# A normalisation turn laid out by feature block: one eviction of 512 or 256 columns in place of four of 128

## The chip, the cores and the metric

One NeuronCore of a Trainium2 chip runs the whole program in one launch. The metric is the device time of that launch in microseconds (us), the median of several runs. Inside the core, TensorE (PE in the profile) multiplies and transposes, VectorE (DVE) and ScalarE (ACT) compute and bring results out of PSUM, GpSimd (POOL) helps, and SyncE (SP) issues most of the DMA transfers. PSUM has eight banks of 512 float32 columns.

## What is computed

Two blocks of a model run behind each other on 512 image tokens and 256 context tokens of width 1024, all in float32. The first block mixes the tokens (a gated delta rule in both directions beside a convolution module) and then sends the image tokens through 64 experts, six for each token. The second block has an RWKV layer and a latent-attention layer. Each of these four layers begins in the same way, and this is the part the change is about:

```python
def rmsnorm(x, g):
    xf = x.astype(jnp.float32)
    y = xf * lax.rsqrt(jnp.mean(xf * xf, axis=-1, keepdims=True) + EPS)
    return (y * g.astype(jnp.float32)).astype(x.dtype)

def modulate(h, shift, scale):
    return h * (1 + scale) + shift

        h_x = rmsnorm_2(x, norm_g[i]) * (1.0 + sc_x) + sh_x
        h_c = rmsnorm_2(ctx, norm_g[i]) * (1.0 + sc_c) + sh_c
```

The inverse length belongs to a token, gain and shift belong to a feature, and the context has a gain and a shift of its own.

## The kernel before, in words

The tokens lie in `K.X` as six tiles of 128 tokens by 1024 features: tiles 0 and 1 are the context, 2 to 5 the image. The layers behind want the features on the partitions, `K.hT[feature in block, block k, token]` with `KD` = 8 blocks of 128 features. `norm_turn` makes the one out of the other. It is called four times: ahead of `mixer_inputs` with six tiles, ahead of `router` with the four image tiles, ahead of `rwkv_heads` with six, and ahead of `mla_inputs` with six. In the views the tile of scaled tokens is `norm_xn`, and the inverse lengths (`known`) were made by the layer before.

The program is a row of phases written by hand. `phase` opens a block in which each engine has a program of its own, and a barrier of all engines stands between two blocks (its branches are the lines L61 and L63 of the views). So nothing of the next phase starts on any engine until the last one has finished the turn. DMAs that SP issued inside a phase go on across the barrier; each turn is given a function `ahead`, which issues the loads for the phase behind it.

The turn before goes tile by tile. DVE multiplies a tile by its inverse lengths (L472) into one of two buffers. PE transposes its eight blocks of 128 by 128 (L497) into two of four banks; a bank then holds four feature blocks of one tile. As gain and shift differ from block to block, each of the eight blocks is evicted by an instruction of its own, 128 columns wide: ACT takes blocks 0 to 3 (L456), DVE blocks 4 to 7 (L483). DVE's order is this:

```python
            scale(0)
            for n, j in enumerate(tiles):
                if n + 1 < N:
                    scale(n + 1)
                r = int(j < JC)
                dve.wait_ge(S["turned"], n + 1)
```

and `scale(n)` waits until the transposes of tile n-2 have given its buffer back. PE waits for the scaled tile and, from the third tile on, for both evictions of the tile two before.

## Time and profile before

| | before |
|---|---|
| median of 3 runs | 2966.68 us (2965.19 to 2973.23) |
| profiled execution, its own time | 2958.97 us |
| its span | 2957.3 us |
| PE busy | 2529.8 us, 86% |
| DVE busy | 1372.4 us, 46% |
| ACT busy | 709.6 us, 24% |
| POOL busy | 458.9 us, 16% |
| HBM read and written | 413.82 and 76.55 MB |

The span is the time between the first and the last instruction of the profiled execution; its own time lies 1.67 us above it. Busy shares are averages over very different layers. What a stretch between two barriers costs is read from its own rows, not from these shares.

### The profile page before, as it was taken

To read this page: it belongs to the slowest core of one execution; us is meant where nothing else is said; L and a number is where in the kernel's file an instruction comes from. 1 tells how busy PE (TensorE), PEld (TensorE's weight loads), DVE (VectorE), ACT (ScalarE), POOL (GpSimd) and SP (SyncE) were. 2 spreads that over 40 slices of the span, in tenths; PEclk is the share of its full clock that TensorE was granted. 3 is DMA by queue.
4 is the path that set the end of the run, shared out by engine and by line. 5 is a ranking of instruction groups with operands and counts; after the bars stand their busy time and mean duration, and the time that the engine had idled before them with its cause. 6 is when DMAs were issued, how large, how long until landed. Compare 5 with 4: busy or idle time off the path is not lost. (4 is left out here: it accounts for less than half of the span.)

```text
span 2957.3 us, 48668 instructions
## 1 busy us (share of the span) xinstructions
PE 2529.8 (86%) x19642; PEld 1482.0 (50%) x19642; DVE 1372.4 (46%) x2761; ACT 709.6 (24%) x1320; POOL 458.9 (16%) x426
## 2 busy tenths in 40 slices
PE   5999773988899998997179999979998499989988
PEld 2554353954444443433045556458887145545553
DVE  1550646533611111111887885966665562034442
ACT  3111340102111111111324641133333113134441
POOL 0000132300111111111000000022211220035450
PEclk8999876998999999999599999999999799999999
DMA  6110611015589999995615655244443932021001
GB/s 250 51 57 1 218 21 27 7 58 183 211 323 394 389 416 404 401 389 212 234 61 145 161 141 173 111 132 133 127 125 84 359 114 95 6 40 18 15 29 64
DMA packets 328930, 471.43 MB, mean 159 GB/s; under 512 B 151465, under 2 KB 225107, under 8 KB 304005
## 3 DMA queue, kind: packets, MB, share of 16 engines
q1 hardware_dynamic: 302645, 373.92, 36.6%
q10 hardware_dynamic: 12960, 69.21, 5.7%
q0 software_dynamic: 13104, 25.19, 2.3%
q8 instruction: 158, 2.59, 0.4%
q14 instruction: 63, 0.52, 0.1%
HBM read 413.82 MB, written 76.55 MB: 166 GB/s over the span
## 5 line engine op out<-in xcount | busy, mean ns | idle before, releaser
L1962 PE MATMUL psum<-ex_w,hT 128*64 128x512 f32 (+1 forms) x1104 | 329.3, 617 | 26.4 <-DMA ex_w<-in_exp_w_up 24.7
L1962 PEld LDWEIGHTS psum<-ex_w,hT 128*64 128x64 f32 (+1 forms) x1104 | 124.9, 158 | 224.6 <-issue 222.5
L4005 POOL TENSOR_SCALAR mla_pool<-mla_pool,at_stats 128x768 f32<-128x768 f32 x64 | 140.2, 2203 | 252.4 <-DVE at_stats L4023 252.4
L2195 DVE COPY slot_act_t<-psum 128x256 f32<-128x256 f32 x45 | 19.1, 424 | 325.2 <-PE psum L1970 325.2
L560 PE MATMUL psum<-hT,weights 128*128 128x512 f32 x384 | 166.8, 592 | 0.0
L1978 PE MATMUL psum<-ex_w,slot_act_t 128*64 128x512 f32 (+1 forms) x552 | 163.4, 597 | 1.4 <-DVE slot_act_t L2195 1.4
L1947 POOL DMA_INDIRECT scratch_ys<-slot_out,slot_row x45 | 45.3, 1006 | 465.3 <-issue 401.6
L560 PEld LDWEIGHTS psum<-hT,weights 128*128 128x128 f32 x384 | 73.0, 190 | 86.6 <-issue 86.0
L2151 ACT ACTIVATE slot_silu<-psum 128x256 f32<-128x256 f32 x45 | 17.3, 384 | 397.6 <-PE psum L1962 397.6
L497 PE MATMUL psum<-const,norm_xn 128*128 128x128 f32 x176 | 30.0, 332 | 91.8 <-DVE norm_xn L472 91.8
L3903 PE MATMUL psum<-mla_kT,at_qT 128*128 128x512 f32 (+1 forms) x256 | 93.3, 489 | 2.6 <-DVE at_qT L4015 1.6
L3179 PE MATMUL psum<-rs_r_ident,rs_b 64*32 64x96 f32 x1536 | 83.8, 249 | 13.6 <-POOL rs_k_ident L3151 12.9
L1978 PEld LDWEIGHTS psum<-ex_w,slot_act_t 128*64 128x64 f32 (+1 forms) x552 | 55.8, 153 | 75.8 <-issue 71.2
L2202 DVE COPY slot_out<-psum 128x512 f32<-128x512 f32 x45 | 31.1, 692 | 128.8 <-PE psum L1978 128.8
L4028 DVE TENSOR_REDUCE at_stats<-psum 128x1 f32<-128x768 f32 x64 | 61.1, 955 | 61.8 <-PE psum L3903 61.6
L3978 ACT ACTIVATE mla_pool<-psum,at_stats 128x768 f32<-128x768 f32 x64 | 57.6, 901 | 127.6 <-DVE at_stats L4033 127.5
L2762 PE MATMUL psum<-rh_w,rh_lerp 128*128 128x256 f32 (+1 forms) x288 | 85.0, 458 | 3.2 <-ACT rh_xx L2837 2.7
L3472 PE MATMUL psum<-ro_wo,ro_oT 128*128 128x512 f32 x192 | 86.4, 608 | 0.9 <-DMA ro_wo<-in_rwkv_w_out 0.9
L2696 PE MATMUL psum<-rh_lerp,rh_w 128*128 128x512 f32 (+1 forms) x256 | 86.2, 490 | 0.0
L3179 PE MATMUL psum<-rs_r_ident,rs_k_ident 64*32 64x96 f32 x1536 | 84.3, 249 | 1.2 <-issue 1.1
L2658 PE MATMUL psum<-rh_lerp,rh_w 128*128 128x512 f32 (+1 forms) x256 | 83.9, 486 | 0.7 <-issue 0.7
L2762 PE MATMUL psum<-tokens,rh_lerp 128*128 128x512 f32 x192 | 82.7, 592 | 0.0
(573 smaller groups left out, 4996.4 us busy)
## 6 DMA issues: line engine op xcount, KB each, us to landing
ex_w<-in_exp_w_gate SPq DMA_DIRECT2D x64, 1024.0 KB, 9.1
ex_w<-in_exp_w_up SPq DMA_DIRECT2D x64, 1024.0 KB, 18.9
ex_w<-in_exp_w_down ACTq DMA_DIRECT2D x60, 1024.0 KB, 10.3
mod_ring<-in_w_mod SPq DMA_DIRECT2D x12, 2048.0 KB, 13.3
scratch_features<-tokens SPq DMA_DIRECT2D x96, 256.0 KB, 3.8
weights<-in_w_in SPq DMA_DIRECT2D x6, 2048.0 KB, 8.1
ex_w<-in_mod_w SPq DMA_DIRECT2D x6, 2048.0 KB, 12.5
ex_w<-scratch_ys SPq DMA_DIRECT2D x8, 1536.0 KB, 18.8
```

The costliest lines, as they stand in the source:

```text
L560: mm = pe.matmul(K.bank[2 * (f % 4)][:, :], K.wring[:, n % RING, k, m * P:(m + 1) * P], K.hT[:, k, TC:TT], start=(k == 0), stop=(k == KD - 1))
L1962: mm = pe.matmul(bank[at:at + n, :], XT[:, k, at:at + n], W[:, 0:2, k * DE:(k + 1) * DE], start=(k == 0), stop=(k == KD - 1))
L1978: mm = pe.matmul(bank[at:at + n, :], aT[:, m, at:at + n], W[:, 2, m * D + h * 512:m * D + (h + 1) * 512], start=(m == 0), stop=(m == 1))
L2658: mm = pe.matmul(K.bank[b][:, 0:t1 - t0], rk_w(s)[:, 1, k, :], lerp[:, 0, k, t0:t1], start=(k == 0), stop=(k == KD - 1))
L2696: mm = pe.matmul(K.bank[2 + seg][:, 0:t1 - t0], rk_w(s)[:, 0, k, :], lerp[:, 1, k, t0:t1], start=(k == 0), stop=(k == KD - 1))
L2762: mm = pe.matmul(K.bank[u % 4][:, 0:cols], lerp[:, n, k, j * P:(j + 1) * P], w[:, k, :], start=(k == 0), stop=(k == KD - 1))
L3179: m = pe.matmul(K.bank[scb(u, k)[p]][sides[p], ch * P:ch * P + W], lhs[p], RI[part, k, ch, :], start=True, stop=True)
L3472: mm = pe.matmul(K.bank[M_[j % 2][half]][:, :], oT[:, j % 2, k, :], wb[:, k, half * 512:(half + 1) * 512], start=(k == 0), stop=(k == KD - 1))
L3903: mm = pe.matmul(K.bank[2 * (u % 2) + b][:, 0:t1 - t0], qT[:, s, h, qt * P:(qt + 1) * P], kT[:, s, h, t0:t1], start=True, stop=True)
L3978: act.activation(Pm[:, q % 2, u, :], K.psum[:, b * 512:b * 512 + TT], ACT.Exp, bias=st[:, 1, u:u + 1], scale=SCALE, accum_out=st[:, 2, u:u ...
L4005: pool.tensor_scalar(Pm[:, q % 2, u, :], Pm[:, q % 2, u, :], st[:, 3, u:u + 1], None, ALU.mult)\
L4028: dve.tensor_reduce(st[:, 0, u:u + 1], K.psum[:, b * 512:b * 512 + TT], AX.X, ALU.max)\
```

## The change

The turn goes by feature blocks. All tiles get a buffer of their own, so that they can be scaled without waiting: DVE scales tiles 0, 2, 4 and ACT tiles 1, 3, 5. PE first transposes the two context tiles into banks 0 to 3, where the two tiles of one feature block stand side by side (256 columns). Then it goes through the eight feature blocks of the image tiles: the four tiles of one block fill one bank (512 columns), in banks 4 to 7 and then 0 to 3, which by then have to be evicted. One instruction evicts one feature block, since all of its columns share gain and shift: 256 columns wide for the context, 512 for the image, half of them on ACT and half on DVE. Three of the calls pass `room`: memory that is unused at that time serves for some or all of the buffers. The branch that computed the inverse lengths within the turn, which no caller used, is gone.

```diff
--- before.py
+++ after.py
@@ -418,20 +418,27 @@
 
 
 
-def norm_turn(K, tiles, gain, shift, known=None, ahead=None):
+def norm_turn(K, tiles, gain, shift, known, ahead=None, room=()):
+
 
 
     nc = K.nc
-    names = "sq_done rms_done inv_done xn_done turned evac_a evac_b"
+    N, ctx = len(tiles), [n for n, j in enumerate(tiles) if j < JC]
+    names = "xn_v xn_a turned evac_v evac_a"
     with ExitStack() as c, phase(nc, names) as (block, S):
-        if known is None:
-            junk = c.enter_context(sbuf(nc, "norm_junk", [P, D], F32))
-            ssq, rms, inv = (c.enter_context(sbuf(nc, "norm_" + n, [P, NT], F32)) for n in ("ssq", "rms", "inv"))
-        xn = c.enter_context(sbuf(nc, "norm_xn", [P, 2, D], F32))
-        N = len(tiles)
-
-        def bank(n, half):
-            return K.bank[2 * (n % 2) + half]
+        xn = list(room)[:N]
+        if len(xn) < N:
+            own = c.enter_context(sbuf(nc, "norm_xn", [P, N - len(xn), D], F32))
+            xn += [own[:, n, :] for n in range(N - len(xn))]
+        parts = [(k, 1) for k in range(KD) if ctx] + [(k, 0) for k in range(KD)]
+        turned = lambda k, r: (k // 2 + 1) * 2 if r else k + 1 + (KD if ctx else 0)
+        on_dve = lambda k, r: (k // 2 if r else k) % 2
+        x_bank = lambda k: (4 + k) % 8
+
+        def source(k, is_ctx):
+            if is_ctx:
+                return K.bank[k // 2][:, (k % 2) * TC:(k % 2 + 1) * TC], K.hT[:, k, 0:TC]
+            return K.bank[x_bank(k)][:, :], K.hT[:, k, TC:TT]
 
         if ahead:
             @block.sync
@@ -440,61 +447,45 @@
 
         @block.scalar
         def _(act):
-            if known is None:
-                for n, j in enumerate(tiles):
-                    if n:
-                        act.wait_ge(S["sq_done"], n)
-                    act.activation(junk[:, :], K.X[:, j, :], ACT.Square, accum_out=ssq[:, n:n + 1])\
-                        .then_inc(S["sq_done"], 1)
-                act.wait_ge(S["sq_done"], N)
-                act.activation(rms[:, 0:N], ssq[:, 0:N], ACT.Sqrt, bias=K.eps[:, :], scale=1.0 / D)\
-                    .then_inc(S["rms_done"], 1)
-            for n, j in enumerate(tiles):
-                r = int(j < JC)
-                act.wait_ge(S["turned"], n + 1)
-                for k in range(KD // 2):
-                    last = act.activation(K.hT[:, k, j * P:(j + 1) * P], bank(n, 0)[:, k * P:(k + 1) * P],
-                                          ACT.Identity, bias=shift[:, k, r:r + 1], scale=gain[:, k, r:r + 1])
-                last.then_inc(S["evac_a"], 1)
+            for n in range(1, N, 2):
+                act.activation(xn[n], K.X[:, tiles[n], :], ACT.Copy, scale=known[:, n:n + 1]).then_inc(S["xn_a"], 1)
+            for k, r in parts:
+                if not on_dve(k, r):
+                    act.wait_ge(S["turned"], turned(k, r))
+                    bank, out = source(k, r)
+                    act.activation(out, bank, ACT.Identity, bias=shift[:, k, r:r + 1], scale=gain[:, k, r:r + 1])\
+                        .then_inc(S["evac_a"], 1)
 
         @block.vector
         def _(dve):
-            if known is None:
-                dve.wait_ge(S["rms_done"], 1)
-                dve.reciprocal(inv[:, 0:N], rms[:, 0:N]).then_inc(S["inv_done"], 1)
-                dve.wait_ge(S["inv_done"], 1)
-            scales = inv if known is None else known
-
-            def scale(n):
-                if n >= 2:
-
-                    dve.wait_ge(S["turned"], n - 1)
-                dve.tensor_scalar(xn[:, n % 2, :], K.X[:, tiles[n], :], scales[:, n:n + 1], None, ALU.mult)\
-                    .then_inc(S["xn_done"], 1)
-
-            scale(0)
-            for n, j in enumerate(tiles):
-                if n + 1 < N:
-                    scale(n + 1)
-                r = int(j < JC)
-                dve.wait_ge(S["turned"], n + 1)
-                for k in range(KD // 2, KD):
-                    q = k - KD // 2
-                    last = dve.tensor_scalar(K.hT[:, k, j * P:(j + 1) * P], bank(n, 1)[:, q * P:(q + 1) * P],
-                                             gain[:, k, r:r + 1], shift[:, k, r:r + 1], ALU.mult, ALU.add)
-                last.then_inc(S["evac_b"], 1)
+            for n in range(0, N, 2):
+                dve.tensor_scalar(xn[n], K.X[:, tiles[n], :], known[:, n:n + 1], None, ALU.mult).then_inc(S["xn_v"], 1)
+            for k, r in parts:
+                if on_dve(k, r):
+                    dve.wait_ge(S["turned"], turned(k, r))
+                    bank, out = source(k, r)
+                    dve.tensor_scalar(out, bank, gain[:, k, r:r + 1], shift[:, k, r:r + 1], ALU.mult, ALU.add)\
+                        .then_inc(S["evac_v"], 1)
 
         @block.tensor
         def _(pe):
-            for n in range(N):
-                pe.wait_ge(S["xn_done"], n + 1)
-                if n >= 2:
-
-                    pe.wait_ge(S["evac_a"], n - 1)
-                    pe.wait_ge(S["evac_b"], n - 1)
+            def ready(n):
+                pe.wait_ge(S["xn_a"] if n % 2 else S["xn_v"], n // 2 + 1)
+
+            for n in ctx:
+                ready(n)
                 for k in range(KD):
-                    half, q = divmod(k, KD // 2)
-                    tr = pe.transpose(bank(n, half)[:, q * P:(q + 1) * P], xn[:, n % 2, k * P:(k + 1) * P], K.ident)
+                    at = (k % 2) * TC + n * P
+                    tr = pe.transpose(K.bank[k // 2][:, at:at + P], xn[n][:, k * P:(k + 1) * P], K.ident)
+                    if n == ctx[-1]:
+                        tr.then_inc(S["turned"], 1)
+            for k in range(KD):
+                if ctx and x_bank(k) < 4:
+                    pe.wait_ge(S["evac_v"] if x_bank(k) % 2 else S["evac_a"], x_bank(k) // 2 * 2 + 2)
+                for q, n in enumerate(range(len(ctx), N)):
+                    if k == 0:
+                        ready(n)
+                    tr = pe.transpose(K.bank[x_bank(k)][:, q * P:(q + 1) * P], xn[n][:, k * P:(k + 1) * P], K.ident)
                 tr.then_inc(S["turned"], 1)
 
 
@@ -2460,7 +2451,7 @@
                 mods.request(I, sp)
 
             norm_turn(K, range(JC, NT), K.mods[:, 1, 0, :, :], K.mods[:, 1, 1, :, :], K.inv,
-                      ahead=ahead)
+                      ahead=ahead, room=[Wb[:, 0, :, :].rearrange("p w n -> p (w n)")[:, n * D:(n + 1) * D] for n in range(JX)])
             router(K, I, wt, kept, R, rw, bias, mods, Wb, shared)
         dispatch(K, wt, kept, w_of, extra, order, h_rows, idx, to_row, Wb, src, acc, mods, K.next_mods,
                  scratch["gate_rows"], steps, Hg, G)
@@ -4074,6 +4065,7 @@
                 ws = sb("ml_w", [P, KD, SMALL], c3)
                 N = held(nc, c3, "w_in g_in0 g_in1")
                 norm_turn(K, range(NT), K.mods[:, 0, 0, :, :], K.mods[:, 0, 1, :, :], K.inv,
+                          room=[pool_[:, (8 + n) * D:(9 + n) * D] for n in range(4)],
                           ahead=lambda sp: load_latents(I, sp, N, ws, gate_weights(pool_)))
                 dump(K, dbg, "hh1", K.hT[:, :, :])
                 qc = pool_[:, 10752:12288].rearrange("p (j n) -> p j n", j=JX)
@@ -4166,7 +4158,9 @@
                     K.hT = sb("hT", [P, KD, TT], c3)
                     K.wring = sb("weights2", [P, RING, KD, WCH], c3)
                     W = held(nc, c3, MIXER_SEMS)
-                    norm_turn(K, range(NT), K.mods[:, 0, 0, :, :], K.mods[:, 0, 1, :, :], inv,
+                    free = [headsT[:, 2 * n:2 * n + 2, :].rearrange("p a t -> p (a t)") for n in range(4)] +\
+                        [cfa[:, 2 * n:2 * n + 2, :].rearrange("p a t -> p (a t)") for n in range(2)]
+                    norm_turn(K, range(NT), K.mods[:, 0, 0, :, :], K.mods[:, 0, 1, :, :], inv, room=free,
                               ahead=lambda sp: [load_mixer(K, I, sp, W, n) for n in range(RING)])
                     dump(K, dbg, "hT", K.hT[:, :, :])
                     mixer_inputs(K, I, C, zT, cfa, cfs, ba[:, :, :], W)
```

The next rows are PE's instructions in the first turn, before the change; `const` is the identity, and what stands in square brackets are the semaphores that the instruction waits for.

```order
L497 MATMUL psum<-const,norm_xn 128x128 [waits xn_done]
L497 MATMUL psum<-const,norm_xn 128x128 x7
L497 MATMUL psum<-const,norm_xn 128x128 [waits xn_done]
L497 MATMUL psum<-const,norm_xn 128x128 x7
L497 MATMUL psum<-const,norm_xn 128x128 [waits evac_b,evac_a,xn_done]
L497 MATMUL psum<-const,norm_xn 128x128 x7
```

The last two rows stand there for each of the tiles 2 to 5. With the change PE has this at the same place (`mix_heads` and `cf_a` are the memory passed as `room`; the buffers of tiles 0 to 3 lie in the first, those of 4 and 5 in the second):

```order
L479 MATMUL psum<-const,mix_heads 128x128 [waits xn_v]
L479 MATMUL psum<-const,mix_heads 128x128 x7
L479 MATMUL psum<-const,mix_heads 128x128 [waits xn_a]
L479 MATMUL psum<-const,mix_heads 128x128 x7
L488 MATMUL psum<-const,mix_heads 128x128 [waits xn_v]
L488 MATMUL psum<-const,mix_heads 128x128 [waits xn_a]
L488 MATMUL psum<-const,cf_a 128x128 [waits xn_v]
L488 MATMUL psum<-const,cf_a 128x128 [waits xn_a]
L488 MATMUL psum<-const,mix_heads 128x128 x2
L488 MATMUL psum<-const,cf_a 128x128 x2
```

There are 48 transposes in both. Before, four of the six groups wait for evictions; now the waits for scaled tiles stand in the first twenty, and the 28 behind them wait only four times, once for each of banks 0 to 3. In the turn with four image tiles the 16 rows of L479 and these four waits are missing.

The next rows are DVE's in the first turn, before the change.

```order
L472 TENSOR_SCALAR norm_xn<-tokens,norm_inv 128x1024 x2
L483 TENSOR_SCALAR hT<-psum,mod_cols 128x128 [waits turned]
L483 TENSOR_SCALAR hT<-psum,mod_cols 128x128 x3
L472 TENSOR_SCALAR norm_xn<-tokens,norm_inv 128x1024 [waits turned]
L483 TENSOR_SCALAR hT<-psum,mod_cols 128x128 [waits turned]
L483 TENSOR_SCALAR hT<-psum,mod_cols 128x128 x3
```

And these are DVE's with the change:

```order
L462 TENSOR_SCALAR mix_heads<-tokens,norm_inv 128x1024 x2
L462 TENSOR_SCALAR cf_a<-tokens,norm_inv 128x1024
L467 TENSOR_SCALAR hT<-psum,mod_cols 128x256 [waits turned] x4
L467 TENSOR_SCALAR hT<-psum,mod_cols 128x512 [waits turned] x4
```

Before, scaling a tile stood behind the eviction of the tile two ahead of it, and DVE had 24 evictions and six scalings. Now its three scalings stand first and wait for nothing, and eight evictions follow. ACT's list changes in the same way: 24 evictions of 128 columns become three scalings, four evictions of 256 columns and four of 512.

## Rows read from the trace of the kernel before

**Rows 1.** Busy time by engine in the four turns, first scaling to last eviction

```profile
core 0: us, PE busy (x) PEld busy (x) DVE busy (x) ACT busy (x) POOL busy (x), PEclk, DMA share, GB/s
60.14:73.48 13.34, 7.66 (x48) 6.49 (x48) 11.81 (x30) 8.91 (x24) 0.00 (x0) 0.87 0.94 338
687.22:696.44 9.22, 5.62 (x32) 4.74 (x32) 7.93 (x20) 6.01 (x16) 0.00 (x0) 0.81 0.50 133
1461.10:1474.45 13.35, 8.31 (x48) 6.97 (x48) 11.81 (x30) 9.02 (x24) 0.00 (x0) 0.79 0.72 167
2467.87:2481.21 13.34, 8.39 (x48) 7.05 (x48) 11.81 (x30) 9.02 (x24) 0.00 (x0) 0.79 0.94 354
```

**Rows 2.** Timeline of the first turn: start, length, engine, line, idle before

```profile
60.14 1.42 DVE L472 TENSOR_SCALAR norm_xn<-tokens,norm_inv 128x1024 f32<-128x1024 f32 x2 [0.84 <-PEq L63]
60.95 3.29 PE L497 MATMUL psum<-const,norm_xn 128*128 128x128 f32 x16 [2.08 <-DVE norm_xn L472]
...
70.85 1.09 PE L497 MATMUL psum<-const,norm_xn 128*128 128x128 f32 x8 [0.84 <-DVE norm_xn L472]
71.98 1.50 ACT L456 ACTIVATE hT<-psum,mod_cols 128x128 f32<-128x128 f32 x4 [0.43 <-PE psum L497]
...
74.32 5.19 PE L556 MATMUL psum<-hT,weights 128*128 128x256 f32 x16 [2.38 <-PEq L63]
```

**Rows 3.** Timeline of PE in the last turn and behind it

```profile
2468.68 3.68 PE L497 MATMUL psum<-const,norm_xn 128*128 128x128 f32 x16 [2.34 <-DVE norm_xn L472]
...
2482.02 18.30 PE L3679 MATMUL psum<-ml_w,hT 128*128 128x384 f32 x56 [2.35 <-PEq L63]
```

**Rows 4.** Stretches in and behind the turns; PEclk is the granted clock's share

```profile
61.00:63.00 2.00, 2.00 (x10) 2.00 (x11) 0.60 (x2) 0.04 (x1) 0.00 (x0) 0.50 0.79 193
64.00:73.00 9.00, 4.61 (x35) 3.44 (x33) 9.00 (x26) 7.38 (x21) 0.00 (x0) 1.00 1.05 392
74.00:77.00 3.00, 2.68 (x6) 2.18 (x7) 0.00 (x0) 0.00 (x0) 0.21 (x4) 0.50 1.05 386
...
2469.00:2473.00 4.00, 3.58 (x17) 3.19 (x16) 2.60 (x8) 2.11 (x6) 0.00 (x0) 0.50 0.93 336
2474.00:2481.00 7.00, 3.48 (x26) 2.57 (x24) 7.00 (x19) 5.80 (x16) 0.00 (x0) 1.00 1.04 409
...
688.50:691.00 2.50, 2.50 (x13) 2.50 (x12) 1.35 (x5) 1.21 (x4) 0.00 (x0) 0.50 0.71 156
...
699.00:709.00 10.00, 10.00 (x49) 10.00 (x49) 0.00 (x0) 1.60 (x3) 0.00 (x0) 0.50 1.03 372
```

**Rows 5.** Groups of instructions by form: count, busy us, mean ns of one

```profile
L2912 DVE TENSOR_SCALAR rh_sq<-psum 128x512 f32<-128x512 f32 x8 | 5.5, 691 | 44.6 <-PE psum L2668 44.6
L2786 ACT ACTIVATE rh_a<-psum,rh_cols 128x512 f32<-128x512 f32 x16 | 11.0, 688 | 0.1
L2379 ACT ACTIVATE junk<-tokens 128x1024 f32<-128x1024 f32 x10 | 10.6, 1057 | 57.7 <-DVE tokens L2425 57.5
```

**Rows 6.** Line L497: ns of one transpose, min/median/max

```profile
L497 PE MATMUL psum<-const,norm_xn x176: 272/273/477, 61.0 to 2479.4; 128*128 128x128 f32 x176
```

**Rows 7.** DMAs that feed the phases behind: KB each, us from issue to landing

```profile
weights<-in_w_in SPq DMA_DIRECT2D x1, 2048.0 KB, 8.1
...
ml_w<-in_mla_w_in SPq DMA_DIRECT2D x1, 2688.0 KB, 9.9
```

**Rows 8.** Timeline behind the second turn (router)

```profile
697.25 12.66 PE L1586 MATMUL psum<-rt_w,hT 128*128 128x64 f32 x64 [2.35 <-PEq L63]
...
697.81 1.28 ACT L1600 ACT_TABLE_LOAD   x1 [1.37 <-POOL ex_w L1576]
```

**Rows 9.** Timeline behind the third turn (RWKV)

```profile
1475.25 0.45 DVE L2877 COPY rh_xx<-hT 128x8 f32<-128x8 f32 x1 [0.94 <-PEq L63]
...
1478.99 5.31 PE L2725 MATMUL psum<-rh_lerp,rh_exps 128*128 128x512 f32 x8 [6.09 <-DVE rh_lerp L2888]
```

**Rows 10.** The costliest group of the page, section 5 (experts)

```profile
L1962 PE MATMUL psum<-ex_w,hT 128*64 128x512 f32 (+1 forms) x1104 | 329.3, 617 | 26.4 <-DMA ex_w<-in_exp_w_up 24.7
```

## The prediction

> **What bounds the kernel now.** I read the stretches of the four turns first. Each turn lies between two barriers, so its length is on the path whatever the busy shares of the whole program say. The three turns of six tiles take 13.34, 13.35 and 13.34 us, that of four takes 9.22 us: 49.3 us, 1.7% of the span [rows 1]. That is the most that the change can touch directly. Inside a turn no engine is at its limit: in the first, PE is busy 7.66 us of 13.34, DVE 11.81, ACT 8.91 [rows 1]. The timeline then shows the loop that sets the pace: eight transposes take 1.09 us, and before them PE was idle for 0.84 us, waiting for DVE to have scaled the tile [rows 2]. So a tile takes 1.93 us, and DVE is the late one: its scaling of a tile stands in its queue behind four evictions of 128 columns. The last eviction, ACT's, starts at 71.98 and ends at 73.48; the next phase's first matmul starts 0.84 us later, at 74.32 [rows 2]. This 0.84 us is the barrier and stays.
>
> **What a turn takes with the change.** Take t as the time since the first scaling starts.
>
> Start: PE starts at 60.95, 0.81 us after DVE [rows 2]; unchanged, as tile 0 is scaled by the same instruction.
>
> Scaled tiles: two scalings on DVE take 1.42 us [rows 2], so tiles 0, 2, 4 are ready at about 0.8, 1.4 and 2.2. ACT's scaling of 1024 columns isn't in the trace; the nearest row is an ACT pass over the same columns out of SBUF, 1.06 us [rows 5], so tiles 1, 3, 5 are ready at 1.1, 2.2 and 3.2. From below it can't be faster than DVE's 0.71, which would change nothing with six tiles. From above, a table load of 1.28 us [rows 8] might come ahead of it; then tile 5 is ready at 4.5. PE needs it after 19 transposes, at 0.81 + 19 x 0.213 = 4.9 at the low clock and at 4.1 if the clock rises as in the first turn. With six tiles that is covered to within 0.4 us; with four it would cost up to 1.3 us. The evictions that ACT runs before go without a load, and I take none.
>
> Transposes: the same 48. One lasts 273 ns at best and 477 at worst [rows 6]. Eight in 1.09 us [rows 2] make (1.09 - 0.27) / 7 = 0.117 us from start to start; sixteen in 3.68 us [rows 3] make (3.68 - 0.48) / 15 = 0.213. The granted clock explains the two: 0.50 (1.2 GHz) from 2469 to 2473 and from 61 to 63, then 1.00 (2.4 GHz) for the rest of the turn [rows 4]. So the clock rose 2 to 3 us after PE's first transpose in the first turn and 4.3 to 5.3 us after it in the last [rows 2 to 4]. What PE does in that time is nearly the same with the change (transposes back to back), and I take the same rises, 2.4 and 4.6 us. The third turn has the same busy times as the last [rows 1] and gets the same number.
>
> Evictions: DVE's 512 columns out of PSUM with scalars took 0.69 us, ACT's with one operand by pointer 0.69 us [rows 5]; ACT's here has two, which I put at up to 0.78. One bank of image columns takes PE 4 x 0.117 = 0.47 us at its fastest, so each engine gets a bank every 0.94 us and keeps up. Nor do PE's four new waits bind: the context banks are full at t = 4.2 at the latest, ACT has taken the first two of its four (under 0.69 us each) by about 4.6, DVE its own by the same time, and PE reaches the first of these banks with transpose 33, at t = 5.6 in the first turn and 6.6 in the others. The last bank is DVE's. The tail is therefore 0.15 us for the last transpose to end and 0.04 + 0.69 for its eviction: 0.88.
>
> Six tiles, third and last turn: 0.81 + 4.6 at the low clock (21.6 transposes) + 26.4 x 0.117 = 3.1 + 0.88 = 9.4 us, 3.9 less than 13.3. First turn: 0.81 + 2.4 (11.3 transposes) + 36.7 x 0.117 = 4.3 + 0.88 = 8.4, 4.9 less. Four tiles: the first bank waits for ACT's second scaling and is full at 2.4; low to about 4.6 (clock 0.50 from 688.5 to 691 [rows 4]), 10 transposes; 18 more take 2.1; with the tail 7.6, 1.6 less than 9.2.
>
> **What the saved time runs into.** The transfers for the next phase are issued as the turn begins and don't get faster. The mixer's first weights land 8.1 us after issue, `ml_w` after 9.9 [rows 7]. The mixer's PE would now start at t = 8.4 + 0.84 = 9.2, 1.1 us after the landing; that of the latent projections at 10.2, 0.3 us after it. Both are still hidden, the second just so: if that turn is shorter than I say, the DMA takes the rest. Behind the third turn DVE has to work first, from 1475.25 to 1478.99, before PE gets its first operand [rows 9], so all of the saving there passes on. The router's matmuls begin as the barrier opens and wait for no DMA [rows 8].
>
> Behind the turns the clock matters too. The mixer's first 16 matmuls took 5.19 us, most of it at 0.50 [rows 2, 4]; PE will have paused for less time, and up to 1.5 us (half of 2.9) may come back. The router's 64 matmuls took 12.66 us [rows 8] at 0.50 [rows 4]; at the transposes' 0.117 they would take 7.5, 5.2 less. The last turn's followers ran at 18.30 / 56 = 0.327 us each, with the clock at 1.00 ahead of them [rows 3, 4], and could lose 1.5 us by a start like the mixer's. I take zero for all three.
>
> **The sum.** 4.9 + 1.6 + 3.9 + 3.9 = 14.3 us. The profiled execution's own 2958.97 us becomes 2944.7. The median of the runs, 2966.68, lies 7.7 above that execution, so in terms of the median I forecast 2952.4. About 0.3%, 8.9 us, is what a measurement of this kernel can tell from no change (its three runs lie 8 us apart).
>
> **Rivals.** (1) The clock never rises in a turn laid out like this. Then 48 transposes take 0.81 + 48 x 0.213 + 0.88 = 11.9 us, 1.4 saved three times, and the four-tile turn takes 2.4 + 28 x 0.213 + 0.88 = 9.2, nothing saved: 4.2 us in all, 2962.5. Against it: from 64 to 73 and from 2474 to 2481 PE ran nothing but transposes, in bursts, and was granted 1.00 [rows 4]. This is what the Trainium skill would have ("TensorE: Matmul & The Clock Gate", section "Part 4: PE-mode transpose"): it says that the full clock does not engage for transposes, because they don't count as work in the same way. By that rule the sum would be 4.2 in place of 14.3; the trace contradicts it. Chance 0.04.
>
> (2) The saving is given back further on. The costliest group, the experts' matmuls, was kept waiting 24.7 us by weights [rows 10]; if the arrival of those didn't move with the start, the 6.5 us of the first two turns would be lost there, which leaves 7.8: 2958.9. Against it: these loads are issued by phases behind the same barriers, which move forward as a whole. Chance 0.13.
>
> (3) More than forecast: the router's stage keeps the high clock and the mixer starts on it. 14.3 + 5.2 + 1.5 = 21, 2945.7. For it: PE is denser before the barrier. Against it: in the router's stage 10 us of unbroken matmuls of 64 columns did not bring the clock up again [rows 4], so it would only be held for a while. Chance 0.13.
>
> (4) Slower: a stream behind a turn stays at 1.2 GHz as the router's did. Only the 56 matmuls behind the last turn are long enough: all of them at half speed cost 18.3 us more, and the change turns into a loss once more than 14.3 us of that stream, four fifths of it, ran low; in full it gives 2970.7. Against it: this stream ran at 0.327 us each from its first matmul, and PE's pause ahead of it gets no longer. Chance 0.03.
>
> **How the numbers follow.** The forecast case, savings of 9 to 18 us, has 0.67. The range of 2945 to 2961 holds it, case 3 and most of case 2; it leaves out cases 1 and 4 and some of the spread of the runs. Faster by over 0.3%: nearly all of the forecast case, case 3 and a little of case 2, 0.80. Within 0.3%: case 1, most of case 2 and the lower edge of the forecast case, 0.17. Slower: 0.03.
>
> **What the profile after would show.** The turns at 8.4, 7.6, 9.4 and 9.4 us from the first scaling to the last eviction; PE without a gap in its transposes from the twentieth on, at 0.117 us each after the clock's rise; evictions of 512 columns at 0.69 to 0.78 us; no ACT_TABLE_LOAD in a turn; the matmuls behind the last turn waiting for no DMA. The prediction is wrong if PE waits for evictions in banks 0 to 3, if the clock rises later than before, or if a phase behind a turn doesn't end earlier by as much as the turn did.

## The result, and the profile after

The changed kernel takes 2945.11 us (median of 10 runs, 2938.78 to 2958.05) where the kernel before takes 2966.17 (10 runs, 2962.28 to 2975.91). The ratio is 0.9927, with a 95% interval of 0.9915 to 0.9938: about 21 us faster. I had forecast 14.3; the median lies at the lowest edge of my range, 2945 to 2961. The profiled execution took 2945.34 us, its span is 2943.6. In three of the later experiments one run of twelve took 5.4 to 8.0 ms, far off all others, and is left out of the ratio.

The four turns in the trace after, from the first scaling to the last eviction, against [rows 1] (columns: length of the stretch, busy us and count of each engine, granted clock, DMA share and GB/s):

```profile
60.02:68.75 8.73, 7.07 (x48) 6.84 (x48) 7.03 (x11) 8.03 (x11) 0.00 (x0) 0.76 0.88 313
683.30:691.34 8.04, 6.11 (x32) 5.29 (x32) 4.65 (x6) 5.27 (x6) 0.00 (x0) 0.66 0.43 100
1451.76:1460.93 9.17, 7.51 (x48) 7.28 (x48) 7.23 (x11) 8.26 (x11) 0.00 (x0) 0.72 1.05 237
2457.70:2467.36 9.66, 8.00 (x48) 7.76 (x48) 7.22 (x11) 8.25 (x11) 0.00 (x0) 0.69 0.90 333
```

They took 13.34, 9.22, 13.35 and 13.34 us before, so the turns themselves give 4.6, 1.2, 4.2 and 3.7, together 13.7 us. PE now works 7.1 to 8.0 us of the 8.7 to 9.7 in the turns of six tiles; DVE has 11 instructions where it had 30.

The groups of the first turn by form (count, busy us, mean ns of one) show the new operations; they answer to [rows 5]:

```profile
L467 DVE TENSOR_SCALAR hT<-psum,mod_cols 128x512 f32<-128x512 f32 x4 | 3.1, 805 | 0.1
L456 ACT ACTIVATE hT<-psum,mod_cols 128x512 f32<-128x512 f32 x4 | 3.0, 782 | 0.2
L456 ACT ACTIVATE hT<-psum,mod_cols 128x256 f32<-128x256 f32 x4 | 1.9, 562 | 0.0
L467 DVE TENSOR_SCALAR hT<-psum,mod_cols 128x256 f32<-128x256 f32 x4 | 1.9, 537 | 1.6 <-PE psum L479 1.6
L451 ACT ACTIVATE cf_a<-tokens,norm_inv 128x1024 f32<-128x1024 f32 x1 | 1.1, 1132 | 0.0
```

What lies behind the turns is the part that I had not counted. The timeline of the changed kernel, behind the first turn, from the second turn's transposes on, and behind the last turn, is to be read beside [rows 2, 8]:

```profile
69.59 3.69 PE L547 MATMUL psum<-hT,weights 128*128 128x256 f32 x16 [1.68 <-PEq L63]
...
685.52 4.98 PE L488 MATMUL psum<-const,ex_w 128*128 128x128 f32 x29 [0.27 <-ACT ex_w L451]
...
692.18 7.33 PE L1577 MATMUL psum<-rt_w,hT 128*128 128x64 f32 x64 [1.68 <-PEq L63]
...
703.88 3.65 PE L246 MATMUL psum<-ex_w 128*64 128x512 f32 x16 [0.79 <-DMA ex_w<-in_mod_w]
...
2468.19 14.11 PE L3670 MATMUL psum<-ml_w,hT 128*128 128x384 f32 x43 [1.68 <-PEq L63]
```

The router's 64 matmuls take 7.33 us where they took 12.66, and the mixer's first 16 take 3.69 where they took 5.19. The stretches of the changed kernel give the reason, against the last rows of [rows 4]: the granted clock is 1.00 (2.4 GHz) through both, where it was 0.50 (1.2 GHz) in nearly all of both.

```profile
684.00:688.00 4.00, 3.62 (x15) 3.03 (x16) 1.52 (x3) 2.51 (x4) 0.00 (x0) 0.50 0.51 112
689.00:691.00 2.00, 1.50 (x14) 1.26 (x12) 1.67 (x3) 1.55 (x2) 0.00 (x0) 1.00 0.49 108
692.00:699.00 7.00, 6.82 (x61) 6.85 (x62) 0.11 (x1) 2.79 (x3) 0.52 (x1) 1.00 1.04 391
69.60:73.00 3.40, 3.40 (x16) 3.01 (x17) 0.00 (x0) 0.00 (x0) 0.16 (x4) 1.00 1.05 386
```

In the trace of before the router's matmuls, from 697.25 on, did not meet a low clock. They met a high one and lost it 1.3 us later:

```profile
697.25:698.55 1.30, 1.30 (x12) 1.30 (x13) 0.11 (x1) 0.74 (x1) 0.48 (x1) 1.00 1.05 405
698.65:709.90 11.25, 11.25 (x56) 11.13 (x55) 0.00 (x0) 1.95 (x3) 0.00 (x0) 0.50 1.03 374
```

To see where the whole difference lies, I split each span into four stretches and the rest. A stretch begins with DVE's first scaling of a turn and ends where the phase behind it has passed the point in question: for the mixer, the start of its first 512-column matmul; for the router, the first matmul of the dispatch phase; for RWKV and the latent projections, their first matmul. In us:

| trace | mixer | router | RWKV | latent | sum | rest of the span |
|---|---|---|---|---|---|---|
| before | 19.2 | 40.9 | 17.9 | 14.1 | 92.2 | 2865.1 |
| before, second trace | 19.8 | 41.2 | 17.9 | 14.1 | 93.0 | 2871.6 |
| changed | 13.1 | 34.1 | 13.9 | 10.5 | 71.7 | 2871.9 |
| changed, second | 13.5 | 34.1 | 14.5 | 10.1 | 72.2 | 2866.0 |
| changed, third | 13.0 | 33.9 | 14.7 | 10.6 | 72.2 | 2871.3 |
| changed, fourth | 13.2 | 33.9 | 13.8 | 9.7 | 70.6 | 2867.3 |

The sums differ by 20 to 22 us, which is the measured gain. The two first spans differ by 13.7 only, because the rest of the program, whose instructions the change doesn't touch, was 7 us shorter in the first trace of before than in the first of the changed kernel. Over the 18 traces of this study the rest lies between 2865.1 and 2876.7.

A part of that rest does answer to the turns. The first 56 matmuls of the latent projections took 18.30 us in all four traces of the changed kernel, at a granted clock of 1.00. In the five traces with the old turn ahead of them they took 18.30, 19.93, 19.99, 21.35 and 21.26 us; only the first trace of before, the one that I had read, had no low clock in them. In the second one the clock was low for their first 3 us:

```profile
2487.90:2491.00 3.10, 3.10 (x5) 1.75 (x6) 1.04 (x6) 0.00 (x0) 1.27 (x1) 0.50 1.05 410
2491.20:2507.00 15.80, 15.80 (x51) 9.33 (x50) 0.00 (x0) 2.88 (x9) 0.00 (x0) 1.00 0.08 29
```

### The profile page after: what moved, and what is told of

Same layout as the page of the kernel before. It is cut to its first block and busy times, and to the rows that moved or that the text cites. A ratio compares the mean times of both kernels' runs of the same rounds, so it can differ in the third digit from the quotient of the medians.

```text
span 2943.6 us, 48528 instructions
## 1 busy us (share of the span) xinstructions
PE 2529.8 (86%) x19642; PEld 1482.2 (50%) x19642; DVE 1355.8 (46%) x2690; ACT 706.8 (24%) x1271; POOL 459.3 (16%) x426
## 5 line engine op out<-in xcount | busy, mean ns | idle before, releaser
L3170 PE MATMUL psum<-rs_r_ident,rs_b 64*32 64x96 f32 x1536 | 84.4, 249 | 13.1 <-POOL rs_k_ident L3142 12.8
L246 PE MATMUL psum<-mod_ring,mod_silu 128*64 128x512 f32 x192 | 54.9, 724 | 31.6 <-DMA mod_ring<-in_w_mod 29.2
```

Of the source, the lines that this page charges most:

```text
L3170: m = pe.matmul(K.bank[scb(u, k)[p]][sides[p], ch * P:ch * P + W], lhs[p], RI[part, k, ch, :], start=True, stop=True)
```

## The experiments

All ratios are to the kernel before, run on the same chip in the same session. A kernel without a ratio had one execution.

**The kernel before again.** No edit.

> The kernel before, unchanged. If the measured ratio of 0.9927 is all of the change, this gives a ratio of 1.000 within 0.001. It also gives a second trace of the kernel before. Theory 1 (the part of the gain that was not forecast is the clock behind the turns): the router's 64 matmuls take 12.7 us again, and the first 16 of the mixer 5.2 us. Rival (the first trace of before was a lucky one, and a usual execution is longer somewhere else): some stretch outside the turns is longer by several us than in the first trace, and the span is nearer 2964 than 2957.

Measured: ratio 1.0000 (0.9988 to 1.0012), span 2964.7. The router's matmuls took 12.58 us:

```profile
701.10 12.58 PE L1586 MATMUL psum<-rt_w,hT 128*128 128x64 f32 x64 [2.34 <-PEq L63]
```

Both sides were right in a part. The clock behind the turn is as low as in the first trace, and the first trace of before was a short one, by 7.4 us, all but 0.8 of it in the rest of the table. So a difference of two spans says little here, and a difference of stretches does.

**The new turn ahead of the router alone, and in the other three places alone.**

```diff
-            norm_turn(K, range(JC, NT), ...
+            norm_turn_before(K, range(JC, NT), ...   # second kernel; the first has the three others so
```

> The new turn ahead of the router alone, the old one in the three turns of six tiles. Theory 1: the turn itself gives 1.2 us and the router's matmuls on the high clock 5.3, together 6.5 us (ratio 0.9978). Rival (the router's clock is chance and does not come with the turn): 1.2 us, ratio 0.9996, and the router's matmuls take 12.7 us in the trace.

> The new turn in the three places with six tiles, the old one ahead of the router. Theory 1: the turns give 4.6 + 4.2 + 3.7 = 12.5 us and the mixer's start 1.5, together 14.0 us (ratio 0.9953); with the run before this it adds up to the change. Rival (savings are given back or multiplied elsewhere): the two ratios don't add up to 0.9927 within 0.002.

Measured: 0.9970 (0.9959 to 0.9982) for the router alone and 0.9948 (0.9932 to 0.9965) for the other three. The two savings, 0.0030 and 0.0052, add up to 0.0082 beside 0.0073 for the change, within their intervals. The router's matmuls took 7.33 us with its own new turn and 12.26 us without it:

```profile
698.57 7.33 PE L1659 MATMUL psum<-rt_w,hT 128*128 128x64 f32 x64 [1.68 <-PEq L63]
```

```profile
696.02 12.26 PE L1659 MATMUL psum<-rt_w,hT 128*128 128x64 f32 x64 [2.35 <-PEq L63]
```

A turn that became 1.5 us shorter (7.69 for 9.22) is worth 8.9 us (3.4 either way), and the stretch by itself 6.8 to 7.1. The rival, that the router's clock doesn't come with the turn, falls.

**Spare matmuls in the old turn of the router.** The kernel before; PE does work in its pauses whose results nobody uses.

```diff
                 tr.then_inc(S["turned"], 1)
+                if N == JX:
+                    for i in range((0, 1, 3, 7)[n]):
+                        pe.matmul(K.bank[7][:, :], K.ident, K.const[:, 0:512], start=True, stop=True)
```

> The kernel before with 11 spare matmuls of 512 columns in PE's idle time of the router's turn (1 behind the second tile, 3 behind the third, 7 behind the last), their results unused. The turn itself stays as long as before, 9.2 us. Theory 1 (a denser PE ahead of the barrier keeps the clock for the router): the 64 matmuls take about 7.3 us instead of 12.7 and the kernel gains about 5 us (ratio 0.998). Rival (what keeps the clock is something else, or the 64-column matmuls lose it anyway): they take 12.7 us and the ratio is 1.000.

```profile
695.11 6.17 PE L501 MATMUL psum<-const 128*128 128x512 f32 x14
702.14 7.33 PE L1589 MATMUL psum<-rt_w,hT 128*128 128x64 f32 x64 [0.86 <-PEq L63]
```

The clock was kept, 7.33 us, but the ratio is 1.0010 (0.9998 to 1.0022). The row above shows my mistake: the last seven matmuls stand there as fourteen and take 6.17 us, 0.88 each. The last eviction ended after 11.6 us instead of 9.2, and PE's spare work held the barrier for longer still: the router's first matmul came 16.9 us after the first scaling (702.14, from 685.26) instead of 10.0. What the stage gained, the turn and the wait for the spare matmuls lost; the stretch is 41.3 us, as long as in the kernel before. I repeated it with three: 256 columns behind the third tile, 512 and 256 behind the last.

> The kernel before with fewer spare matmuls in the router's turn, since in the run with 11 of them each took 0.88 us and the turn got 2.3 us longer: now one of 256 columns behind the third tile and one of 512 and one of 256 behind the last, results unused. Theory 1 (the clock behind the turn is decided by how busy PE is ahead of the barrier): the turn takes 9.2 to 9.5 us and the 64 router matmuls 7.3 us, ratio 0.998. Rival (so little work is not enough, or it was the shorter pause ahead of the stage): the matmuls take 12.6 us, ratio 1.000.

```profile
695.32 1.46 PE L501 MATMUL psum<-const 128*128 128x512 f32 x4
697.83 7.33 PE L1589 MATMUL psum<-rt_w,hT 128*128 128x64 f32 x64 [1.05 <-PEq L63]
```

The turn took 9.47 us, the matmuls 7.33, and the router's stretch 34.7 us instead of 41.2. So an old turn with a busier PE, and with a pause of 1.05 us instead of 2.35, gives the stage behind it the same clock as the new one. Which of the two did it, this run doesn't tell. The ratio is 0.9990 (0.9978 to 1.0001). That is 3 us (0 to 6.5) where the stretch says 6.5: at the edge of the interval, so the mechanism is shown by the trace, its worth in the median only roughly.

**A buffer for every tile and scaling on two engines, in the old layout.**

```diff
-            scale(0)
+            for n in range(0, N, 2):
+                dve.tensor_scalar(xn[n], K.X[:, tiles[n], :], known[:, n:n + 1], None, ALU.mult).then_inc(S["xn_v"], 1)
             for n, j in enumerate(tiles):
-                if n + 1 < N:
-                    scale(n + 1)
...
```

(against the kernel before; ACT scales tiles 1, 3, 5 in the same way, and PE waits for the scaled tiles of either)

> A buffer for every tile and scaling on both engines up front, as in the change, but the old layout in PSUM with 128-column evictions tile by tile. Theory 1 (the layout with wide evictions and the early scaling are both needed): DVE and ACT then work 12 and 8 evictions less nothing, that is each engine still has 24 evictions of 0.32 to 0.375 us behind its three scalings; ACT is the last with 3.2 + 24 x 0.375 = 12.2 us, a turn of six takes 12.3 us, 1.1 less than before, and half of the gain behind the turns may come: ratio 0.998. Rival (the loop scale, transpose, evict was the whole cost): turns of 9.5 us, ratio 0.993.

Turns of 11.56, 8.47, 12.10 and 11.55 us, ratio 0.9990 (0.9979 to 1.0000). The router's 64 matmuls took 11.90 us, so their clock was lost as before. ACT's row in the last turn shows the new pace: it evicts without a pause, 0.35 us for each 128 columns, while PE waits for it.

```profile
2469.90 8.45 ACT L449 ACTIVATE hT<-psum,mod_cols 128x128 f32<-128x128 f32 x24
```

**The new layout with evictions of 128 columns.**

```diff
-                    act.activation(out, bank, ACT.Identity, ...).then_inc(S["evac_a"], 1)
+                    for at in range(0, TC if r else TX, P):
+                        last = act.activation(out[:, at:at + P], bank[:, at:at + P], ACT.Identity, ...)
+                    last.then_inc(S["evac_a"], 1)
```

(and the same on DVE)

> The changed kernel, but each feature block is evicted by instructions of 128 columns again (two for the context, four for the image), on the same engine as with the change. Theory 1: each engine has 24 of them behind its three scalings, the turn of six tiles ends at about 12.2 us as in the run with the old layout, the one of four at 2.2 + 16 x 0.375 = 8.2 to 8.6; PE waits for evictions in banks 0 to 3. Ratio to before 0.998. Rival: the evictions hide behind PE at the low clock and the ratio is that of the change, 0.993.

Turns of 11.72, 9.64, 11.72 and 11.73 us, ratio 0.9988 (0.9977 to 1.0000). The last turn's rows on PE and ACT:

```profile
2483.82 0.38 PE L492 MATMUL psum<-const,norm_xn 128*128 128x128 f32 x2
2488.94 3.54 PE L3674 MATMUL psum<-ml_w,hT 128*128 128x384 f32 x5 [4.75 <-PEq L63]
```

```profile
2479.66 8.48 ACT L457 ACTIVATE hT<-psum,mod_cols 128x128 f32<-128x128 f32 x24
```

PE is through at 2484.2 and then stands for 4.75 us; ACT's 24 evictions end at 2488.1. I had expected PE to be held up in banks 0 to 3; it was not, the evictions only come out behind it. The start of the latent projections after so long a pause is slow as well, 0.7 us for each of five. The router's matmuls took 13.65 us. Both experiments scale ahead and evict 128 columns at a time; they differ in the layout. Early scaling is thus worth about 3 us by the median with either layout (7 to 8 us by the four stretches with the old one, 2 to 3 with the new one; they add up to 85.1 and 90.2 us), and widening the evictions on top of it brings the gain to 21. Wide evictions without the early scaling were not run: one bank takes a block of four tiles, so those tiles have to be scaled first.

**All scaling on DVE.**

```diff
-            for n in range(1, N, 2):
-                act.activation(xn[n], K.X[:, tiles[n], :], ACT.Copy, scale=known[:, n:n + 1]).then_inc(S["xn_a"], 1)
...
-            for n in range(0, N, 2):
+            for n in range(N):
                 dve.tensor_scalar(xn[n], K.X[:, tiles[n], :], known[:, n:n + 1], None, ALU.mult).then_inc(S["xn_v"], 1)
```

> The changed kernel with all tiles scaled by DVE. Theory 1 (the scaling on ACT is hidden): DVE scales six tiles in 4.1 us, tile 5 is ready at 4.1 us where PE needs it at 4.9, so the turns of six tiles change by less than 0.3 us; DVE's evictions then start 2 us later, up to 0.5 us more at the end. In the turn of four the last tile is ready at 2.8 instead of 2.2, 0.2 us more. Ratio 0.993 within 0.001. Rival (the two-engine scaling is a main part of the gain): turns 2 us longer, ratio 0.996.

Turns of 9.75, 9.76, 9.63 and 8.75 us, ratio 0.9952 (0.9939 to 0.9965), above the 0.993 that I had expected to within 0.001. The turns of six tiles are 1.0 and 0.5 us longer and 0.9 shorter than in the first trace of the change; four traces of the change scatter by as much, from 8.7 to 9.9 us, so I can't tell them apart. The turn of four is 1.7 us longer instead of 0.2, and the router's matmuls took 12.75 us:

```profile
685.34 6.12 PE L486 MATMUL psum<-const,ex_w 128*128 128x128 f32 x29 [0.19 <-DVE ex_w L460]
693.15 12.75 PE L1575 MATMUL psum<-rt_w,hT 128*128 128x64 f32 x64 [1.68 <-PEq L63]
```

```profile
684.00:690.00 6.00, 5.61 (x24) 5.03 (x25) 2.90 (x4) 2.29 (x3) 0.00 (x0) 0.50 0.41 83
691.00:693.00 2.00, 0.46 (x4) 0.22 (x2) 0.81 (x1) 0.75 (x1) 0.00 (x0) 1.00 1.00 383
695.00:705.00 10.00, 10.00 (x49) 10.00 (x49) 0.00 (x0) 1.50 (x2) 0.00 (x0) 0.50 1.04 382
```

The clock rose only as the turn was nearly over (0.50 to 690, 1.00 from 691), and was down again from 695 on. The pause ahead of the stage is 1.68 us, the same as in the change. So keeping the clock isn't certain with the new layout, and I looked at the changed kernel again.

> The changed kernel unchanged. In six traces so far the router's matmuls took 7.3 us in the new turn's trace and in the run with that turn alone, but 12.8 us in the run with scaling on DVE alone, which has the same layout. Theory 1 (the new turn keeps the clock for the router every time): 7.3 us again, ratio 0.9927. Rival (the clock's change falls now before, now behind the barrier, so the router's stage is fast in some executions and slow in others): some of the three looks at this kernel show 12 to 13 us. The ratio is 0.992 to 0.994 in either case.

> Second look at the changed kernel. Theory 1: router matmuls 7.3 us. Rival: 12 to 13 us in at least one of the three.

> Third look at the changed kernel. Theory 1: router matmuls 7.3 us. Rival: 12 to 13 us in at least one of the three.

Measured: 0.9907 (0.9891 to 0.9924), and 7.33 us for the router's matmuls in all three looks, which makes four of four; their stretches are in the table above. The rival falls for this kernel.

**Spare matmuls ahead of two turns.** The changed kernel, with PE busy just ahead of them.

```diff
+            if delta:                        # at the end of the output projection, ahead of the router's turn
+                for i in range(4):
+                    pe.matmul(K.bank[7][:, :], K.ident, K.const[:, 0:512], start=True, stop=True)
...
+        @block.tensor                        # in the combine phase, ahead of RWKV's turn
+        def _(pe):
+            pe.wait_ge(S["gated"], 2 * JX)
+            for i in range(5):
+                pe.matmul(K.bank[7][:, :], K.ident, K.const[:, 0:512], start=True, stop=True)
```

> The changed kernel with spare matmuls of 512 columns (results unused) ahead of two turns: four at the end of the output projection, ahead of the router's turn, and five in the combine phase, ahead of RWKV's, where PE had nothing to do for 72 us. Theory (the first 16 to 20 transposes of a turn cost 0.213 us instead of 0.11 because PE was idle before): the RWKV turn takes 7.5 us instead of 9.2 and the router's 6.5 instead of 8.0, 3.2 us in all, ratio to before 0.9915. Rival (the pause of 1.7 us across the barrier loses the clock again): turns as in the changed kernel, 0.9927.

The two turns took 6.45 and 7.70 us, as expected, with 16 transposes in 1.97 us instead of 3.67:

```profile
1453.10 1.97 PE L479 MATMUL psum<-const,norm_xn 128*128 128x128 f32 x16 [1.96 <-DVE norm_xn L462]
...
1464.73 5.11 PE L2725 MATMUL psum<-rh_lerp,rh_exps 128*128 128x512 f32 x8 [5.80 <-DVE rh_lerp L2888]
```

But the ratio is 0.9913 (0.9897 to 0.9929) beside 0.9907 for the changed kernel in the same session: no gain that can be told. The four stretches add up to 70.9 us, beside 70.6 to 72.2. The router's stretch was 34.7 us in spite of a turn 1.5 us shorter. PE's row there shows where it went, for the second of the three weight chunks had to be waited for, 2.1 us where it was 0.8 to 1.1 in the traces of the changed kernel, and the chunk was then worked off partly at the low clock:

```profile
703.39 5.35 PE L246 MATMUL psum<-ex_w 128*64 128x512 f32 x16 [2.10 <-DMA ex_w<-in_mod_w]
```

**What keeps the clock: the pause or the work.** Four more single looks: the kernel with scaling on DVE again; the changed kernel with the last bank of the router's turn evicted by four instructions, which lengthens PE's pause, twice; and scaling on DVE with one spare matmul in the pause.

```diff
+                    w = P if not ctx and k == KD - 1 else TC if r else TX      # the longer pause
+                    for at in range(0, TC if r else TX, w):
...
+            if not ctx:                                                         # the spare matmul
+                pe.wait_ge(S["evac_a"], 1)
+                pe.matmul(K.bank[4][:, :], K.ident, K.const[:, 0:512], start=True, stop=True)
```

> Second look at the kernel with scaling on DVE alone, where the router's 64 matmuls took 12.75 us after the same pause of 1.68 us as in the change. Theory 1 (the clock is kept when it has risen early enough in the turn; in the first look it rose 2 us ahead of the router's first matmul, in the change 3 to 4 us): 12 to 13 us again if the rise is as late, 7.3 us if it is earlier. Rival (only the length of the pause counts): no fixed relation.

> The changed kernel, but in the router's turn the last bank is evicted by four instructions of 128 columns, which makes the turn 0.5 to 0.6 us longer and PE's pause ahead of the router 2.3 us instead of 1.7, as long as before. Theory 1 (the work of PE in the turn decides): 7.3 us still. Rival (the pause decides): 12 to 13 us.

> Scaling on DVE alone, with one spare matmul of 512 columns (result unused) behind the last transposes of the router's turn, which shortens PE's pause from 1.7 to 0.8 us. If PE's work up to the barrier decides: router matmuls 7.3 us. Rival (what matters is how early the clock rose): 12 to 13 us.

> Second look at the changed kernel with the longer pause ahead of the router. Both looks at 7.3 us: the pause of 2.3 us does not lose the clock by itself. Any look at 12 to 13 us: it can.

The rows of the router's matmuls, in the order of these four:

```profile
695.78 12.69 PE L1575 MATMUL psum<-rt_w,hT 128*128 128x64 f32 x64 [1.68 <-PEq L63]
```

```profile
692.97 7.33 PE L1580 MATMUL psum<-rt_w,hT 128*128 128x64 f32 x64 [2.24 <-PEq L63]
```

```profile
694.16 7.33 PE L1578 MATMUL psum<-rt_w,hT 128*128 128x64 f32 x64 [0.86 <-PEq L63]
```

```profile
691.56 7.33 PE L1580 MATMUL psum<-rt_w,hT 128*128 128x64 f32 x64 [2.24 <-PEq L63]
```

The bracket gives PE's idle time in front. With 2.24 us, nearly the 2.35 of before, the clock was kept twice; with 1.68 us it was lost in both looks at the kernel with scaling on DVE. So the length of the pause alone doesn't decide it. With one more matmul it was kept there, but that also shortened the pause to 0.86 us.

Is it PE's work ahead of the stage, then? These are the last 5 us before the router's first matmul, of the kernel before, the change, and scaling on DVE:

```profile
692.25:697.25 5.00, 1.82 (x16) 1.37 (x14) 4.06 (x12) 3.76 (x11) 0.04 (x1) 1.00 0.67 213
687.18:692.18 5.00, 3.32 (x23) 3.11 (x22) 2.94 (x4) 2.33 (x3) 0.04 (x1) 0.84 0.48 141
688.15:693.15 5.00, 3.32 (x19) 3.11 (x17) 2.43 (x3) 1.74 (x3) 0.04 (x1) 0.72 0.76 259
```

PE was busy 1.82 us of the 5 where the clock was lost, and 3.32 where it was kept, but also 3.32 where it was lost with scaling on DVE. So PE's busy time there doesn't sort the traces alone either.

## Why the prediction was too small

I forecast 14.3 us and measured about 21. The turns came out as forecast; the phases behind them, which I had put at nothing, gave the rest.

**The loop and what ends it: right.** The turn before was paced by scale, transpose, evict in DVE's queue. Scaling ahead with evictions of 128 columns leaves a turn of six tiles at 11.6 to 12.1 us in either layout, with ACT's 24 evictions setting the pace; with wide evictions as well it takes 8.7 to 9.9 in the four traces. So behind the limit that I had named, DVE's queue, a second one lay close, and the change removes both.

**The turns: right in sum.** Forecast 8.4, 7.6, 9.4 and 9.4 us, measured 8.73, 8.04, 9.17 and 9.66; savings of 13.7 us where I had 14.3. Within that, DVE's eviction of 512 columns took 0.81 us instead of 0.69 (the row I had priced it by has its two scalars as immediates, this one reads them by pointer), and ACT's 0.78 as bounded. ACT's scaling took 1.13 us instead of 1.06, with no table load, and PE waited for no eviction. In the first turn the clock rose later than before (where it stayed at 0.50 for less than 2.9 us), one of the signs against me that I had named: it stayed at 0.50 for 3.3 us from PE's first transpose at 60.83, where I had taken 2.4, and the turn is 0.3 us longer than forecast. The clock rose during the transposes in every turn of the changed kernel, so the first rival falls. The third turn shows it best, because PE had been idle for 72 us ahead of it:

```profile
1452.57 3.67 PE L479 MATMUL psum<-const,norm_xn 128*128 128x128 f32 x16 [72.48 <-DVE norm_xn L462]
...
1457.00:1460.00 3.00, 3.00 (x29) 2.84 (x27) 2.71 (x4) 2.66 (x4) 0.00 (x0) 1.00 1.17 303
```

With it goes, for this case, the rule of the Trainium skill ("TensorE: Matmul & The Clock Gate", section "Part 4: PE-mode transpose") that transposes don't bring the full clock: the granted clock was 1.00 from 1457 to 1460, with PE on nothing but transposes since its idle time.

**The DMAs: right.** No matmul at the start of a phase waited for its weights; even the latent projections' first matmul was released by the barrier (L63 in its row).

**The clock behind the turns: the step that failed.** It reads "I take zero for all three." The stretches give for the router's stage 5.3 us in its own matmuls, from 12.66 to 7.33, and for the mixer's start 1.5 us. These were in the prediction, priced at 5.2 and 1.5, but as the third rival with a chance of 0.13, and not in the sum. 13.7 + 5.3 + 1.5 = 20.5, against stretches that differ by 20 to 22. (Behind the router's matmuls the next 16 took 4.83 us in the trace of before and 3.65 with the change; one more wait for weights, below, takes 0.8 of that back.) The third zero, for the latent projections, was wrong in the same direction: I had feared a loss there, and it is the kernel before that has one, 1.6 to 3.1 us in four of five traces. The mixer's 1.5 us is the least certain: its 16 matmuls took 3.69 us in every trace with the new turn, but with the old one 5.19, 5.10, 6.65 and 5.38 us and once 3.69 as well, so now and then the old turn keeps the clock too.

My reason against the router's 5.2 us was that 10 us of unbroken 64-column matmuls at the low clock had not brought it up. That was true, but it says nothing of whether the clock falls at all behind a denser turn. I had read the 12.66 us as low from the first matmul on. In fact the granted clock was 1.00 from 692.25 until 1.3 us into them. In all 18 traces the router's matmuls began at 1.00; in seven the clock fell 0.3 to 2.2 us later and stayed low to their end (11.90 to 13.65 us), and in eleven it stayed at 1.00 for all of their 7.33 us.

**Given back further on: wrong, as forecast.** The two halves of the change add up within their intervals, and the stretches account for the gain of the medians. The rest of the span scatters by 11.6 us over 18 traces, too much to show by itself a loss of the 6.5 us that I had priced. In the router's phase PE now waits some 0.8 us for each of two weight chunks, where it waited for one before; that is all that I found.

What decides that PE's clock survives the barrier is shown only as far as the experiments go. The new turn ahead of the router kept it in all eight traces with scaling on both engines and wide evictions; the old turn lost it in all three without spare matmuls and kept it in both with them; the two kernels with early scaling and evictions of 128 columns lost it, and so did scaling on DVE, twice, until a spare matmul was added. None of three simple readings sorts all of these. The pause alone doesn't (1.68 us lost, 2.24 us kept), and PE's busy time in the last 5 us doesn't (3.32 us both kept and lost). Nor does the time since the clock's rise: it had risen 2 us ahead of the router's matmuls with scaling on DVE (lost), 3 to 4 us with the new turn (kept), and over 5 us in the kernel before (lost). What sorts them stays open.

## What to carry to other kernels

When a turn between two barriers gets denser on PE, ask what the clock does in the phase behind it, and put that into the sum: here a third of the gain lay there, in instructions that the change doesn't touch. Where two limits lie close together (a queue that makes one engine wait, and an engine that has just enough to do), price them together: here the early scaling alone showed a seventh of the gain in the median. A clock read in one stretch says nothing of the matmuls ahead of it, so read it at the first instruction of a phase, and in more than one trace. And when the effect is 1% of the program, compare stretches between fixed points in several traces; two whole spans differed by 7 us for reasons elsewhere.

## What the runs showed of the hardware

- A stream of 64-column matmuls with 128x128 weights began at 2.4 GHz in every trace. Where the clock fell in its first 0.3 to 2.2 us, it ran on at 1.2 GHz for over 10 us without raising it (12.66 us for 64, trace of before); elsewhere it ran at 2.4 GHz to its end (7.33 us).
- With PE idle for 72 us before and then on float32 transposes alone, the granted clock rose from 0.50 to 1.00 (third turn of the change).
- A float32 matmul of 512 columns stands in the trace as two, 0.44 us each at the high clock (fourteen for seven in 6.17 us), and a transpose of 128x128 as one, 0.11 us from start to start (sixteen in 1.97 us).
- An eviction of 512 columns with two operands by pointer took 0.81 us on DVE and 0.78 on ACT in the changed kernel, one of 128 columns 0.40 and 0.46 in the kernel before: four times the columns for about twice the time.
